# A 16-column projection in a two-block network kernel: rounded and low weight parts held side by side in one stationary tile

## The chip, the cores and the metric

The kernel runs on one core of one Trainium2 chip. The metric is device time in microseconds for one execution. Three executions of the kernel before took 2244.69, 2244.84 and 2245.06 us, so the median is 2244.84 us.

## What is computed

The reference runs two blocks over 512 tokens of width 1024. The first has two layers (Fourier and neighbourhood attention, a gated convolution, cross attention to a memory, a convolutional feed-forward part). The second has retention, a gated delta rule and a feed-forward part. The change touches only the two smallest of the second block's projections, `db` and `da`, 8 columns each:

```python
u = rmsnorm(h, g_mix[l])
proj = u @ w_in[l]
(..., db, da, gate_r, gate_d) = jnp.split(proj, split_at, axis=-1)
...
g = -jnp.exp(dn_a_log[l]) * jax.nn.softplus(da.astype(jnp.float32) + dn_dt_bias[l])
beta = jax.nn.sigmoid(db.astype(jnp.float32))
do = gated_delta_chunkwise(cq, ck, cv, g, beta)
```

`g` is summed up inside each chunk of 128 tokens, and its exponentials and `beta` weigh keys, queries and values in the delta rule.

## The kernel before

**Products.** Activations lie feature by token (128 x 512 tiles, eight of them for width 1024). Each fp32 product is made of three products of reduced operands: rounded weights by rounded activations, rounded weights by low activations, low weights by rounded activations. For activations the two parts are XH and XL, for weights w_hi and w_lo. One product is a weight load of 128 x 128 and a matmul that streams 512 tokens.

**Weights.** They come in units of 128 x 1024 floats through a ring of five slots. For each unit, in program order on each engine, SyncE loads w_raw when the unit five before it has been used (semaphore w_used, L492), ScalarE rounds it to w_hi (`split`, L689), and GpSimd subtracts to get w_lo (`lo`, L602; semaphore lo_done). TensorE waits on lo_done and runs `products`: 4 output tiles x 2 weight tiles x 3 products, 24 per unit (L1224).

**The projection.** Between the retention branch and the delta rule stands one unit named "dab". Its 128 stationary columns are 32 columns from `db` on, 32 from `da` on and 64 others, for each of eight weight tiles. Only columns 0 to 7 and 32 to 39 are read later. TensorE runs 8 x 3 products on it (L1841) into bank 0 of PSUM (tile ps) and counts w_used.

**The rows.** VectorE's `decay_rows` (L2284 to L2307) scales the two groups of 8 rows by the norm R, adds dt_bias, and with ScalarE's `decay_rows` (L1014 to L1026) makes beta (BR), the running sum GR of the decay, and two rows derived from it. ScalarE writes GR and BR to DRAM (L1027, L1028), waits until they have landed, and issues a load that spreads them over all 128 partitions (GB, `spread`, L1008). TensorE transposes the rows to columns in `decay_columns` (L1764), three units into the next group.

**The start of the delta rule.** TensorE goes on with four units for the keys (bank group A), four for the queries (bank group B), then `squares` (L1604), which needs ScalarE's SQk. VectorE's order there is fixed in code: `ages(0)` (L2348, L2352; needs GB), `evacuate(0)` (L2324), `with_beta(0)` (L2360), sixteen convolution taps on the keys (L2338, L2341), `ages(1)`, `evacuate(1)`. ScalarE follows with silu of the keys (L1051) and their squares SQk (L1055). The same order comes again for the second half of the heads, without the row computation.

Nothing is scheduled by a planner. Each engine's order is the order of the code, and semaphore values are written out by hand.

Of the kernel before, what the change touches and what calls it, by code (L numbers as in the profile page):

```python
# [18 lines left out]
F32 = mybir.dt.float32  # L19
F32R = mybir.dt.float32r  # L20
ACT = mybir.ActivationFunctionType
ALU = mybir.AluOpType
AX = mybir.AxisListType

P = 128
D = 1024
KT = D // P
T = 512
# [5 lines left out]
RING = 5  # L34
# [17 lines left out]
DN_H = 8  # L52
# [35 lines left out]
HALF = P // 2  # L88
# [6 lines left out]
def program(nc, ins, out):  # L95
    ctx = ExitStack()
    with ctx:
# [8 lines left out]
        XH = sb("XH", [P, KT, T], F32R)  # L106
        XL = sb("XL", [P, KT, T], F32R)
        w_raw = sb("w_raw", [P, RING, 2, UC])
        w_lo = nc.alloc_sbuf_tensor_at("w_lo", [P, RING, 2, UC], F32R, offset=nc.sbuf_base - RING * 2 * UC * 4)
        w_hi_at = nc.sbuf_base  # L110
        w_hi = sb("w_hi", [P, RING, 2, UC], F32R)
        R = sb("R", [P, T])
# [14 lines left out]
        ps = ctx.enter_context(nc.psum_tensor("ps", [P, 8, T], F32))  # L127

        def at(name, kb, shape, dt=F32):

            return nc.alloc_sbuf_tensor_at(name, shape, dt, offset=a0 + int(kb * KB))
# [36 lines left out]
        def pcol(name, i=0, n=1):  # L168
            c = PARAM_COLS[name][0] + i
            return par[:, c:c + n]  # L170
# [82 lines left out]
        SQo, LNo = at("SQo", 48, [P, 4, T]), at("LNo", 56, [P, 4, T])  # L253
        SQL, SQH = at("SQL", 48, [P, 4, T], F32R), at("SQH", 56, [P, 4, T], F32R)
        EGA = at("EGA", 88, [P, 4, T])
        GB = at("GB", TL + 25.5, [P, 2, 2, T])
        KD = at("KD", TL + 25.5, [P, 4, T])
        PKM, PKT = at("PKM", 64, [P, 4 * NCH, FIRST]), at("PKT", 65, [P, 4 * NCH, FIRST])
# [335 lines left out]
        def _(pool):  # L594
# [3 lines left out]
            def lo(u):  # L598

                s = u % RING  # L600
                pool.wait_ge(hi_done, u)
                nc.gpsimd.tensor_tensor(w_lo[:, s, :, :], w_raw[:, s, :, :], w_hi[:, s, :, :].bitcast(F32),  # L602
                                        ALU.subtract).then_inc(lo_done, 1)

# [77 lines left out]
        def _(act):  # L682
# [327 lines left out]
            def decay_rows():  # L1010

                B1, A1, A3, SPR, BEG, EGL, EG8 = [rows[i][:, :] for i in (0, 1, 2, 3, 4, 5, 6)]
                act.wait_ge(ab_dve, 1)
                nc.scalar.activation(BR[:, :], B1, ACT.Sigmoid).then_inc(ab_act, 1)  # L1014
                act.wait_ge(ab_dve, 3)
                nc.scalar.activation(A3, A1, ACT.Abs).then_inc(ab_act, 1)
                act.wait_ge(ab_act, 2)
                nc.scalar.activation(A3, A3, ACT.Exp, scale=-1.0).then_inc(ab_act, 1)
                act.wait_ge(ab_act, 3)
                nc.scalar.activation(A3, A3, ACT.Ln, bias=1.0).then_inc(ab_act, 1)  # L1020
                nc.scalar.activation(sm[0:DN_H, 80:81], pcol("a_log")[0:DN_H, :], ACT.Exp).then_inc(ab_act, 1)
                split_to(first["dab"] + 2 + LEAD)
                act.wait_ge(ab_dve, 9)
                nc.scalar.activation(EG8, GR[:, :], ACT.Exp).then_inc(ab_act, 1)
                act.wait_ge(ab_dve, 14)
                nc.scalar.activation(EGL, EGL, ACT.Exp).then_inc(ab_act, 1)  # L1026
                nc.scalar.dma_start(rows_dram[0], GR[:, :]).then_inc(rows_saved, 16)  # L1027
                nc.scalar.dma_start(rows_dram[1], BR[:, :]).then_inc(rows_saved, 16)  # L1028
                spread(0)
                split_to(first["dab"] + 3 + LEAD)  # L1030
                act.wait_ge(ab_t, 1)
                nc.scalar.activation(TC[:, :, :, :], ps[:, 1, 0:4 * NCH * DN_H].rearrange("p (a n h) -> p a n h", a=4, n=NCH),
                                     ACT.Copy).then_inc(ab_act, 1)
# [175 lines left out]
        def _(pe):  # L1209
# [547 lines left out]
            def decay_columns():  # L1757

                pe.wait_ge(ab_act, 7)
                pe.wait_ge(ab_dve, 14)  # L1760
                for a, row in enumerate((BR, GR, rows[4], rows[5])):
                    for n in range(NCH):
                        o = (a * NCH + n) * DN_H
                        mm = nc.tensor.transpose(ps[:, 1, o:o + DN_H], row[:, n * P:(n + 1) * P], ident[0:DN_H, 0:DN_H])  # L1764
                mm.then_inc(ab_t, 1)
# [55 lines left out]
            def block2():  # L1821
                u0 = first["rqk"]
                group(u0, 4, 0, XH, XL, x_ready("rqk"), after=stats("rqk"))
                stat_read("rqk")
                pe.wait_ge(bn_dve, 3)
                group(u0 + 4, 4, 4, XH, XL)
                for g in range(2):
                    pe.wait_ge(rqk_out, g + 1)
                    group(first["rv"] + 4 * g, 4, 4 * g, XH, XL, tokens_out=True)
                retention()  # L1830
                pair("gater", [[(ret_sc, 4 * RET_H)], [(ret_ro, 8)]])
                pair("retbr", [[(gr_dve, 1)], [(gr_dve, 2)]], YH, YL, lambda kt: [(rg_dve, 2 * (kt // 4) + 4)])

                u = first["dab"]
                pe.wait_ge(lo_done, u + 1)
                pe.wait_ge(rb_dve, 1)
                hi = w_hi[:, u % RING, :, :].rearrange("p a (b c) -> p (a b) c", c=P)
                lo = w_lo[:, u % RING, :, :].rearrange("p a (b c) -> p (a b) c", c=P)
                for kt in range(KT):
                    for n, (a, b) in enumerate(((hi, XH), (hi, XL), (lo, XH))):  # L1840
                        mm = nc.tensor.matmul(ps[:, 0, :], a[:, kt, :], b[:, kt, :], start=kt == 0 and n == 0,  # L1841
                                              stop=kt == KT - 1 and n == 2)
                mm.then_inc(w_used, 1)
                delta(0)
                delta(1)
                pair("dz", [[], [(do_ln, 2)]], after=out_stats(1))
                pair("dnbr", [[(dz_dve, 1)], [(dz_dve, 4)]], YH, YL, lambda kt: [(dz_dve, 3 * (kt // 4) + 3)])
                pair("wo2", [[(dn_dve, 1)], [(dn_dve, 4)]], NH, NL, lambda kt: [(dn_dve, 3 * (kt // 4) + 3)])
                ffn2()
                last_stats()  # L1850
# [5 lines left out]
        def _(dve):  # L1856
# [423 lines left out]
            def decay_rows():  # L2280
                B1, A1, A3, SPR, BEG, EGL, EG8, ONE = [rows[i][:, :] for i in range(8)]
                step = lambda n: dve.wait_ge(ab_dve, n)
                dve.wait_ge(w_used, first["dab"] + 1)
                nc.vector.tensor_tensor(B1, ps[0:DN_H, 0, :], R[0:DN_H, :], ALU.mult).then_inc(ab_dve, 1)  # L2284
                nc.vector.tensor_tensor(A1, ps[32:32 + DN_H, 0, :], R[32:32 + DN_H, :], ALU.mult).then_inc(ab_dve, 1)
                step(2)
                nc.vector.tensor_scalar(A1, A1, pcol("dt_bias")[0:DN_H, :], None, ALU.add).then_inc(ab_dve, 1)
                nc.vector.memset(ONE, 1.0)

                dve.wait_ge(ab_act, 4)  # L2290
                step(3)
                nc.vector.scalar_tensor_tensor(out=SPR, in0=A1, scalar=0.0, in1=A3, op0=ALU.max,
                                               op1=ALU.add).then_inc(ab_dve, 1)
                dve.wait_ge(ab_act, 5)
                step(4)
                nc.vector.tensor_scalar(SPR, SPR, sm[0:DN_H, 80:81], -1.0, ALU.mult, ALU.mult).then_inc(ab_dve, 1)
                step(5)
                for n in range(NCH):
                    c = slice(n * P, (n + 1) * P)
                    nc.vector.tensor_tensor_scan(GR[:, c], ONE[:, c], SPR[:, c], 0.0, ALU.mult, ALU.add).then_inc(ab_dve, 1)  # L2300
                step(9)
                for n in range(NCH):
                    c = slice(n * P, (n + 1) * P)
                    nc.vector.tensor_scalar(EGL[:, c], GR[:, c], GR[:, (n + 1) * P - 1:(n + 1) * P], -1.0,
                                            ALU.subtract, ALU.mult).then_inc(ab_dve, 1)
                dve.wait_ge(ab_act, 6)
                nc.vector.scalar_tensor_tensor(out=BEG, in0=EG8, scalar=-1.0, in1=BR[:, :], op0=ALU.mult,  # L2307
                                               op1=ALU.mult).then_inc(ab_dve, 1)
# [348 lines left out]
def lay_out(inputs):  # L2657
# [5 lines left out]
         "ret_g": feat(a["ret_norm_g_2"][0]), "dn_conv": feat(a["dn_conv_w_2"][0]), "dn_g": feat(a["dn_norm_g_2"][0]),  # L2663
         "ffn_w2": feat(a["ffn_conv_w_2"][0]), "ffn_b2": feat(a["ffn_conv_b_2"][0]),
         "a_log": np.pad(a["dn_a_log_2"].T, ((0, P - DN_H), (0, 0))),
         "dt_bias": np.pad(a["dn_dt_bias_2"].T, ((0, P - DN_H), (0, 0)))}
    for l in range(2):
        f[f"mix{l}"] = feat(a["mix_norm_g"][l])
        f[f"xa{l}"] = feat(a["xa_norm_g"][l])
# [9 lines left out]
    for n in WEIGHTS:  # L2679
# [5 lines left out]
WEIGHTS = ("w_in_ab", "w_out_ab", "w_in_c", "w_out_c", "xa_wq", "xa_wkv", "xa_wo", "ffn_w_up", "ffn_w_down",  # L2685
           "w_in_2", "w_ret_br_2", "w_dn_br_2", "w_o_2", "w_up_2", "w_down_2")
C_DB, C_DA, C_GR, C_GD = 7168, 7176, 7184, 8208
LOG_GAMMA = [float(np.log(1.0 - 2.0 ** (-5.0 - h))) for h in range(RET_H)]
SCALE_NA = float(P) ** -0.5
SCALE_X = float(2 * P) ** -0.5  # L2690
# [27 lines left out]
```

## Time and profile before

| quantity | value |
|---|---|
| median of three executions | 2244.84 us |
| span of the profiled execution | 2243.1 us |
| TensorE busy | 2224.7 us, 99% |
| VectorE, ScalarE, GpSimd busy | 952.6, 873.2, 1016.2 us |
| mean granted TensorE clock | 0.999 |
| waits of TensorE on the chain | 5% of the span is on other engines |

The span goes from the first to the last instruction of one profiled execution. The profile gives no other time for that execution; the median of the timed ones is 1.7 us longer than the span. A busy share says how much of the span the engine had an instruction under way. The chain of waits is followed back from the last instruction, each step to what released it.

### The profile page before, as it was taken

The numbers are of one execution on the slowest core, as the hardware profiler recorded it, in microseconds if no ns is written. First come the engines' busy times: TensorE is split into PE (matmuls) and PEld (weight loads), VectorE is DVE, ScalarE is ACT, GpSimd is POOL, SyncE is SP. The second block draws the span as 40 slices with busy tenths as digits, with TensorE's granted clock in tenths as the row PEclk, the third lists the DMA queues.
The fourth block names the chain that finished last, engine by engine and source line by source line (L and its number), as shares of the span: only waits on it lengthen the run. The fifth ranks groups of instructions, "written<-read, shape, count | busy, mean of one in ns | idle before, by whom it ended". The sixth has DMA issues, their size and how long they took to land.

```text
span 2243.1 us, 25574 instructions
## 1 busy us (share of the span) xinstructions
PE 2224.7 (99%) x10856; PEld 1836.8 (82%) x10856; DVE 952.6 (42%) x1171; ACT 873.2 (39%) x1080; POOL 1016.2 (45%) x431
## 2 busy tenths in 40 slices
PE   9999999999999999999999999999999999999998
PEld 7888878888888887888888877888878888888887
DVE  6251225342143403253414634168587224666603
ACT  4354334232322443332334536255664534332222
POOL 5427334444444472355443632434333454465643
PEclk9999999999999999999999999999999999999999
DMA  6215223323332341233233431344241233333322
GB/s 236 98 60 167 75 66 96 102 94 94 101 96 94 114 151 47 94 95 102 94 108 99 127 85 47 99 129 100 62 117 48 85 132 96 101 94 95 102 94 76
DMA packets 161090, 222.86 MB, mean 99 GB/s; under 512 B 24256, under 2 KB 87744, under 8 KB 160720
## 3 DMA queue, kind: packets, MB, share of 16 engines
q1 hardware_dynamic: 159136, 216.08, 31.0%
q10 hardware_dynamic: 1840, 5.15, 0.7%
q8 instruction: 86, 1.41, 0.3%
q14 instruction: 28, 0.23, 0.0%
HBM read 214.34 MB, written 6.85 MB: 99 GB/s over the span
## 4 chain that ended last, share of the span: by engine, by line
PE 95%; DVE 3%; ACT 1%; issue 0%; DMA 0%; POOL 0%; SPq 0%; DVEq 0%; ACTq 0%
PE ps L1224 82%; PE ps L1448 2%; PE ps L1461 1%; PE ps L1486 1%; PE ps L1445 1%; PE ps L1574 1%; PE ps L1310 1%; PE ps L1604 1%; PE ps L1563 0%; DVE ACC L1865 0%; PE ps L1619 0%; PE ps L1582 0%; PE ps L1631 0%; PE ps L1612 0%; PE ps L1474 0%
## 5 line engine op out<-in xcount | busy, mean ns | idle before, releaser
L602 POOL TENSOR_TENSOR w_lo<-w_raw,w_hi 128x1024 fp32r<-128x1024 f32 x378 | 972.8, 2583 | 1187.5 <-ACT w_hi L689 1172.1
L689 ACT ACTIVATE w_hi<-w_raw 128x1024 fp32r<-128x1024 f32 x378 | 396.2, 1056 | 885.2 <-DMA w_raw<-w_in 124.6
L1224 PE MATMUL ps<-XH,w_hi 128*128 128x512 f32 x1760 | 688.5, 391 | 0.0
L1224 PE MATMUL ps<-XH,w_lo 128*128 128x512 f32 x1760 | 685.0, 389 | 0.0
L1224 PE MATMUL ps<-XL,w_hi 128*128 128x512 f32 x1760 | 684.8, 389 | 0.0
L1224 PE MATMUL ps<-HID,w_hi 128*128 128x512 f32 x1728 | 533.1, 390 | 0.1
L1224 PEld LDWEIGHTS ps<-XH,w_hi 128*128 128x128 f32 x1760 | 330.4, 188 | 69.5 <-issue 1.2
L1224 PEld LDWEIGHTS ps<-XH,w_lo 128*128 128x128 f32 x1760 | 330.3, 188 | 69.3
L1224 PEld LDWEIGHTS ps<-XL,w_hi 128*128 128x128 f32 x1760 | 330.4, 188 | 68.8 <-issue 1.2
L1224 PEld LDWEIGHTS ps<-HID,w_hi 128*128 128x128 f32 x1728 | 324.2, 188 | 68.4 <-issue 1.0
L1224 PE MATMUL ps<-HID,w_lo 128*128 128x512 f32 x864 | 336.1, 389 | 0.0
L1224 PEld LDWEIGHTS ps<-HID,w_lo 128*128 128x128 f32 x864 | 162.2, 188 | 33.8
L1889 DVE TENSOR_TENSOR H<-ps,H 128x512 f32<-128x512 f32 x60 | 39.7, 683 | 307.9 <-PE ps L1224 307.9
L2132 DVE TENSOR_TENSOR GP<-ps,R 128x1024 f32<-128x1024 f32 x16 | 19.6, 1225 | 176.3 <-PE ps L1224 176.3
L2083 DVE TENSOR_TENSOR QX<-ps,R 128x2048 f32<-128x2048 f32 x4 | 9.2, 2292 | 156.4 <-PE ps L1224 156.4
L1865 DVE TENSOR_TENSOR ACC<-ACC,SQ 128x512 f32<-128x512 f32 x59 | 48.1, 815 | 42.1 <-ACT SQ L699 38.2
L2520 DVE SCALAR_TENSOR_TENSOR CV<-GP,par,CV 128x512 f32<-128x512 f32 x88 | 65.7, 817 | 0.0
L2512 DVE TENSOR_TENSOR GP<-ps,R 128x2048 f32<-128x2048 f32 x11 | 25.2, 2292 | 75.8 <-PE ps L1224 75.8
L912 ACT ACTIVATE EG<-CV,par 128x512 f32<-128x512 f32 x32 | 22.2, 725 | 85.6 <-DVE CV L2141 85.6
L699 ACT ACTIVATE SQ<-H 128x512 f32<-128x512 f32 x52 | 32.8, 631 | 32.3 <-DVE ACC L1865 21.9
L2141 DVE SCALAR_TENSOR_TENSOR CV<-GP,par,CV 128x512 f32<-128x512 f32 x64 | 43.6, 740 | 0.0
L2150 DVE TENSOR_TENSOR HID<-HF,HID 128x1024 fp32r<-128x1024 f32 x16 | 35.5, 2221 | 18.1 <-ACT HID L916 18.1
(398 smaller groups left out, 2228.5 us busy)
## 6 DMA issues: line engine op xcount, KB each, us to landing
w_raw<-w_in SPq DMA_DIRECT2D x72, 512.0 KB, 3.8
w_raw<-ffn_w_up SPq DMA_DIRECT2D x128, 256.0 KB, 2.9
w_raw<-w_up SPq DMA_DIRECT2D x88, 256.0 KB, 3.0
w_raw<-xa_wkv SPq DMA_DIRECT2D x32, 512.0 KB, 3.7
w_raw<-ffn_w_down SPq DMA_DIRECT2D x32, 512.0 KB, 3.8
w_raw<-w_in_c SPq DMA_DIRECT2D x24, 512.0 KB, 3.8
w_raw<-w_down SPq DMA_DIRECT2D x22, 512.0 KB, 3.7
w_raw<-xa_wq SPq DMA_DIRECT2D x16, 512.0 KB, 3.8
```

The lines of the kernel that those rows point to most:

```text
L602: nc.gpsimd.tensor_tensor(w_lo[:, s, :, :], w_raw[:, s, :, :], w_hi[:, s, :, :].bitcast(F32), ALU.subtract).then_inc(lo_done, 1)
L689: nc.scalar.activation(w_hi[:, s, :, :], w_raw[:, s, :, :], ACT.Copy).then_inc(hi_done, 1)
L699: nc.scalar.activation(ACC[:, :] if c == 0 else SQ[:, :], H[:, c, :], ACT.Square).then_inc(sq_done, 1)
L1224: mm = nc.tensor.matmul(ps[:, bank + m, :], a, b, start=start and j == 0 and n == 0, stop=stop and j == 1 and n == 2)
L1310: mm = nc.tensor.matmul(ps[:, m, :], wt, (XL if n == 1 else XH)[:, kt, :], start=False, stop=k == 3 and n == 2 and j == 1)
L1448: mm = nc.tensor.matmul(ps[:, bank + m, :], xt[:, m * P:(m + 1) * P], wt, start=begin, stop=end)
L1865: nc.vector.tensor_tensor(ACC[:, :], ACC[:, :], SQ[:, :], ALU.add).then_inc(acc_done, 1)
L1889: nc.vector.tensor_tensor(H[:, c, :], ps[:, (c + flip) % 8, :], H[:, c, :], ALU.add).then_inc(h_upd, 1)
L2141: nc.vector.scalar_tensor_tensor(out=CV[:, q, :], in0=GP[:, q, i:T + i], scalar=tap(i, q), in1=CV[:, q, :], op0=ALU.mult, op1=ALU.add).the ...
L2150: nc.vector.tensor_tensor(HID[:, 2 * g + nf:2 * g + nf + 2, :], HF[:, :, :], HID[:, 2 * g:2 * g + 2, :].bitcast(F32), ALU.subtract).then_i ...
L2512: nc.vector.tensor_tensor(GP4[:, :, 2:T + 2], banks(bank), over(R[:, :], 4), ALU.mult).then_inc(up2_dve, 1)
L2520: nc.vector.scalar_tensor_tensor(out=CV4[:, q, :], in0=GP4[:, q, i:T + i], scalar=of(w0 + 2 * nf * i, q), in1=CV4[:, q, :], op0=ALU.mult, ...
```

## The change

GpSimd no longer writes w_lo for the unit "dab". It subtracts only for the first 64 columns of each of the eight weight tiles, and writes the result into columns 64 to 127 of w_hi, over rounded weights that nobody reads. TensorE then runs two products per weight tile, XH and XL, over the 128 columns of w_hi: rows 0 to 39 of ps hold the rounded weights' share, rows 64 to 103 the low weights' share. The product of low weights by low activations, left out before, is now included. VectorE scales both groups of 40 rows (ABL, ABH) and adds them: `db` by a tensor_tensor, `da` together with dt_bias by a scalar_tensor_tensor that takes the place of the tensor_scalar. dt_bias moves to partitions 32 to 39 of the parameter tile. Every later value of the semaphore ab_dve grows by one, and ScalarE's sigmoid waits for the third VectorE step where it waited for the first.

```diff
+        ABH, ABL = at("ABH", 80, [DAB_ROWS, T]), at("ABL", 82, [DAB_ROWS, T])
...
                 pool.wait_ge(hi_done, u)
+                if u == first["dab"]:
+                    raw, hi = [w[:, s, :, :].rearrange("p a (b c) -> p (a b) c", c=P) for w in (w_raw, w_hi)]
+                    nc.gpsimd.tensor_tensor(hi[:, :, HALF:P], raw[:, :, 0:HALF], hi[:, :, 0:HALF].bitcast(F32),
+                                            ALU.subtract).then_inc(lo_done, 1)
+                    return
...
-                act.wait_ge(ab_dve, 1)
+                act.wait_ge(ab_dve, 3)
                 nc.scalar.activation(BR[:, :], B1, ACT.Sigmoid).then_inc(ab_act, 1)
-                act.wait_ge(ab_dve, 3)
+                act.wait_ge(ab_dve, 4)
                 nc.scalar.activation(A3, A1, ACT.Abs).then_inc(ab_act, 1)
...
-                hi = w_hi[:, u % RING, :, :].rearrange("p a (b c) -> p (a b) c", c=P)
-                lo = w_lo[:, u % RING, :, :].rearrange("p a (b c) -> p (a b) c", c=P)
+                both = w_hi[:, u % RING, :, :].rearrange("p a (b c) -> p (a b) c", c=P)
                 for kt in range(KT):
-                    for n, (a, b) in enumerate(((hi, XH), (hi, XL), (lo, XH))):
-                        mm = nc.tensor.matmul(ps[:, 0, :], a[:, kt, :], b[:, kt, :], start=kt == 0 and n == 0,
-                                              stop=kt == KT - 1 and n == 2)
+                    for n, x in enumerate((XH, XL)):
+                        mm = nc.tensor.matmul(ps[:, 0, :], both[:, kt, :], x[:, kt, :], start=kt == 0 and n == 0,
+                                              stop=kt == KT - 1 and n == 1)
...
-                nc.vector.tensor_tensor(B1, ps[0:DN_H, 0, :], R[0:DN_H, :], ALU.mult).then_inc(ab_dve, 1)
-                nc.vector.tensor_tensor(A1, ps[32:32 + DN_H, 0, :], R[32:32 + DN_H, :], ALU.mult).then_inc(ab_dve, 1)
+                low = slice(HALF, HALF + DAB_ROWS)
+                nc.vector.tensor_tensor(ABL[:, :], ps[low, 0, :], R[low, :], ALU.mult).then_inc(ab_dve, 1)
+                nc.vector.tensor_tensor(ABH[:, :], ps[0:DAB_ROWS, 0, :], R[0:DAB_ROWS, :], ALU.mult).then_inc(ab_dve, 1)
                 step(2)
-                nc.vector.tensor_scalar(A1, A1, pcol("dt_bias")[0:DN_H, :], None, ALU.add).then_inc(ab_dve, 1)
+                nc.vector.tensor_tensor(B1, ABH[0:DN_H, :], ABL[0:DN_H, :], ALU.add).then_inc(ab_dve, 1)
+                nc.vector.scalar_tensor_tensor(out=A1, in0=ABH[32:DAB_ROWS, :], scalar=pcol("dt_bias")[32:DAB_ROWS, :],
+                                               in1=ABL[32:DAB_ROWS, :], op0=ALU.add, op1=ALU.add).then_inc(ab_dve, 1)
                 nc.vector.memset(ONE, 1.0)
```

On TensorE, from the last products of the retention branch (HID) into the unit "dab" and the second weight tile of it, the order before is this:

```order
L1224 MATMUL ps<-HID,w_lo 128x512
L1841 MATMUL ps<-XH,w_hi 128x512 [waits rb_dve,lo_done]
L1841 MATMUL ps<-XL,w_hi 128x512
L1841 MATMUL ps<-XH,w_lo 128x512
L1841 MATMUL ps<-XH,w_hi 128x512
L1841 MATMUL ps<-XL,w_hi 128x512
```

and now:

```order
L1230 MATMUL ps<-HID,w_lo 128x512
L1846 MATMUL ps<-XH,w_hi 128x512 [waits rb_dve,lo_done]
L1846 MATMUL ps<-XL,w_hi 128x512
L1846 MATMUL ps<-XH,w_hi 128x512
L1846 MATMUL ps<-XL,w_hi 128x512
```

The product with w_lo is gone from each of the eight weight tiles; what stands ahead of the unit, what follows it and what it waits for are as before.

On VectorE, from the last product of the retention branch's gate (MG) to the first chunk of the running sum, the order before is this (row_144 is the `db` row, row_145 the `da` row):

```order
L2571 TENSOR_TENSOR MG<-MG,ps 128x2048 [waits gr_act,w_used] x2
L2284 TENSOR_TENSOR row_144<-ps,R 8x512 [waits w_used]
L2285 TENSOR_TENSOR row_145<-ps,R 8x512
L2287 TENSOR_SCALAR row_145<-row_145,par 8x512 [waits ab_dve]
L2288 MEMSET row_151 8x512
L2292 SCALAR_TENSOR_TENSOR row_147<-row_145,row_146 8x512 [waits ab_dve,ab_act]
L2296 TENSOR_SCALAR row_147<-row_147,sm 8x512 [waits ab_dve,ab_act]
L2300 SCALAR_TENSOR_TENSOR GR<-row_151,row_147 8x128 [waits ab_dve]
```

and now (row_146 is the `db` row, row_147 the `da` row):

```order
L2579 TENSOR_TENSOR MG<-MG,ps 128x2048 [waits gr_act,w_used] x2
L2290 TENSOR_TENSOR ABL<-ps,R 40x512 [waits w_used]
L2291 TENSOR_TENSOR ABH<-ps,R 40x512
L2293 TENSOR_TENSOR row_146<-ABH,ABL 8x512 [waits ab_dve]
L2294 SCALAR_TENSOR_TENSOR row_147<-ABH,par,ABL 8x512
L2296 MEMSET row_153 8x512
L2300 SCALAR_TENSOR_TENSOR row_149<-row_147,row_148 8x512 [waits ab_dve,ab_act]
L2304 TENSOR_SCALAR row_149<-row_149,sm 8x512 [waits ab_dve,ab_act]
L2308 SCALAR_TENSOR_TENSOR GR<-row_153,row_149 8x128 [waits ab_dve]
```

The `db` row was ready after the first of three instructions and the `da` row after the third; now they are ready after the third and the fourth of four.

## Rows read from the trace of the kernel before

**Rows 1.** The page: span, and busy time of each engine with its instruction count.

```profile
span 2243.1 us, 25574 instructions
PE 2224.7 (99%) x10856; PEld 1836.8 (82%) x10856; DVE 952.6 (42%) x1171; ACT 873.2 (39%) x1080; POOL 1016.2 (45%) x431
```

**Rows 2.** The page: the chain that ended last, by engine.

```profile
PE 95%; DVE 3%; ACT 1%; issue 0%; DMA 0%; POOL 0%; SPq 0%; DVEq 0%; ACTq 0%
```

**Rows 3.** Chain of waits, 1440 to 1560 us: start, duration, what.

```profile
1455.83 5.44 PE ps L1841 x24
1461.27 16.32 PE ps L1224 x72
1477.59 1.08 PE ps L1764 x16
1478.67 27.43 PE ps L1224 x120
```

**Rows 4.** Timeline of GpSimd, the unit dab: start, duration, line, tiles, idle before and releaser.

```profile
1440.00 2.39 POOL L602 TENSOR_TENSOR w_lo<-w_raw,w_hi 128x1024 fp32r<-128x1024 f32 x1 [4.10 <-ACT w_hi L689]
```

**Rows 5.** Timeline of VectorE, 1455 to 1512 us.

```profile
1455.87 2.29 DVE L2571 TENSOR_TENSOR MG<-MG,ps 128x2048 f32<-128x2048 f32 x1 [19.47 <-PE ps L1224]
1461.31 0.68 DVE L2284 TENSOR_TENSOR row<-ps,R 8x512 f32<-8x512 f32 x1 [3.15 <-PE ps L1841]
1462.02 0.68 DVE L2285 TENSOR_TENSOR row<-ps,R 8x512 f32<-8x512 f32 x1
1462.73 0.63 DVE L2287 TENSOR_SCALAR row<-row,par 8x512 f32<-8x512 f32 x1
...
1482.91 1.04 DVE L2348 TENSOR_TENSOR DL<-GB,TC 128x512 f32<-128x512 f32 x1 [2.22 <-DMA GB<-rows_dram]
1483.98 0.69 DVE L2352 SCALAR_TENSOR_TENSOR DL<-DL,cst 128x512 f32<-128x512 f32 x1
1484.59 0.69 DVE L2348 TENSOR_TENSOR DL<-GB,TC 128x512 f32<-128x512 f32 x1
...
1493.57 7.96 DVE L2341 SCALAR_TENSOR_TENSOR KN<-ps,par,KN 128x511 f32<-128x511 f32 x12
...
1506.14 2.29 DVE L2324 TENSOR_TENSOR H<-ps,R 128x2048 f32<-128x2048 f32 x1 [1.96 <-PE ps L1224]
```

**Rows 6.** Timeline of ScalarE and its DMA issues, 1455 to 1604 us.

```profile
1475.02 0.63 ACT L1026 ACTIVATE row<-row 8x512 f32<-8x512 f32 x1 [0.87 <-DVE row L2307]
...
1477.06 0.40 ACTq L1008 DMA_DIRECT2D GB<-rows_dram  x1
...
1501.56 1.92 ACT L1051 ACTIVATE KN<-KN 128x2048 f32<-128x2048 f32 x1 [5.66 <-DVE KN L2341]
1503.51 1.92 ACT L1055 ACTIVATE SQk<-KN 128x2048 f32<-128x2048 f32 x1
...
1531.82 1.92 ACT L1055 ACTIVATE SQq<-QN 128x2048 f32<-128x2048 f32 x1
```

**Rows 7.** Timeline of TensorE's weight loads in three stretches.

```profile
1505.71 0.42 PEld L1604 LDWEIGHTS ps<-SQk,cst 128*128 128x128 f32 x2
...
1534.54 0.42 PEld L1604 LDWEIGHTS ps<-SQq,cst 128*128 128x128 f32 x2
...
1571.32 0.54 PEld L1646 LDWEIGHTS ps<-MM,AT 64*64 64x64 f32 x16 [0.92 <-DVE MM L2458]
```

**Rows 8.** Timeline of VectorE, 1508 to 1604 us.

```profile
1557.43 0.69 DVE L2428 TENSOR_TENSOR ATT<-ps,DL 128x512 f32<-128x512 f32 x1 [0.91 <-PE ps L1631]
...
1570.82 0.45 DVE L2458 STREAM_TRANSPOSE MM<-MTP 128x256 f32<-128x256 f32 x1
```

**Rows 9.** SyncE's issue of the weights nearest to GB's.

```profile
1477.62 0.37 SPq L492 DMA_DIRECT2D w_raw<-w_in  x1
```

**Rows 10.** All four loads of GB (L1008): issue to landing.

```profile
DMA to landing us min/median/max: 4.9/6.1/7.2
```

**Rows 11.** The stretch from 1482 us on: busy shares, granted clock, DMA share, GB/s.

```profile
1482.00:1483.00 1.00, 1.00 (x6) 0.84 (x5) 0.09 (x1) 0.09 (x1) 1.00 (x1) 1.00 0.94 367
```

More of the change, by code:

```diff
@@ L1022, in decay_rows @@
                 split_to(first["dab"] + 2 + LEAD)
-                act.wait_ge(ab_dve, 9)
+                act.wait_ge(ab_dve, 10)
                 nc.scalar.activation(EG8, GR[:, :], ACT.Exp).then_inc(ab_act, 1)
-                act.wait_ge(ab_dve, 14)
+                act.wait_ge(ab_dve, 15)
                 nc.scalar.activation(EGL, EGL, ACT.Exp).then_inc(ab_act, 1)
@@ L1759, in decay_columns @@
                 pe.wait_ge(ab_act, 7)
-                pe.wait_ge(ab_dve, 14)
+                pe.wait_ge(ab_dve, 15)
                 for a, row in enumerate((BR, GR, rows[4], rows[5])):
@@ L2283, in decay_rows @@
                 dve.wait_ge(w_used, first["dab"] + 1)
-                nc.vector.tensor_tensor(B1, ps[0:DN_H, 0, :], R[0:DN_H, :], ALU.mult).then_inc(ab_dve, 1)
-                nc.vector.tensor_tensor(A1, ps[32:32 + DN_H, 0, :], R[32:32 + DN_H, :], ALU.mult).then_inc(ab_dve, 1)
+                low = slice(HALF, HALF + DAB_ROWS)
+                nc.vector.tensor_tensor(ABL[:, :], ps[low, 0, :], R[low, :], ALU.mult).then_inc(ab_dve, 1)
+                nc.vector.tensor_tensor(ABH[:, :], ps[0:DAB_ROWS, 0, :], R[0:DAB_ROWS, :], ALU.mult).then_inc(ab_dve, 1)
                 step(2)
-                nc.vector.tensor_scalar(A1, A1, pcol("dt_bias")[0:DN_H, :], None, ALU.add).then_inc(ab_dve, 1)
+                nc.vector.tensor_tensor(B1, ABH[0:DN_H, :], ABL[0:DN_H, :], ALU.add).then_inc(ab_dve, 1)
+                nc.vector.scalar_tensor_tensor(out=A1, in0=ABH[32:DAB_ROWS, :], scalar=pcol("dt_bias")[32:DAB_ROWS, :],
+                                               in1=ABL[32:DAB_ROWS, :], op0=ALU.add, op1=ALU.add).then_inc(ab_dve, 1)
                 nc.vector.memset(ONE, 1.0)
                 dve.wait_ge(ab_act, 4)
-                step(3)
+                step(4)
                 nc.vector.scalar_tensor_tensor(out=SPR, in0=A1, scalar=0.0, in1=A3, op0=ALU.max,
@@ L2294, in decay_rows @@
                 dve.wait_ge(ab_act, 5)
-                step(4)
+                step(5)
                 nc.vector.tensor_scalar(SPR, SPR, sm[0:DN_H, 80:81], -1.0, ALU.mult, ALU.mult).then_inc(ab_dve, 1)
-                step(5)
+                step(6)
                 for n in range(NCH):
@@ L2300, in decay_rows @@
                     nc.vector.tensor_tensor_scan(GR[:, c], ONE[:, c], SPR[:, c], 0.0, ALU.mult, ALU.add).then_inc(ab_dve, 1)
-                step(9)
+                step(10)
                 for n in range(NCH):
@@ L2665, in lay_out @@
          "a_log": np.pad(a["dn_a_log_2"].T, ((0, P - DN_H), (0, 0))),
-         "dt_bias": np.pad(a["dn_dt_bias_2"].T, ((0, P - DN_H), (0, 0)))}
+         "dt_bias": np.pad(a["dn_dt_bias_2"].T, ((32, P - 32 - DN_H), (0, 0)))}
     for l in range(2):
@@ L2687 @@
 C_DB, C_DA, C_GR, C_GD = 7168, 7176, 7184, 8208
+DAB_ROWS = 32 + DN_H
 LOG_GAMMA = [float(np.log(1.0 - 2.0 ** (-5.0 - h))) for h in range(RET_H)]
```

## The prediction, on record before the changed kernel ran

> **What bounds the kernel.** I read the page first. TensorE is busy 99% of the span, no other engine over half of it [rows 1], and the chain that ended last runs on TensorE for 95% of the span [rows 2]. So the kernel is as long as TensorE's stream, and a change pays by what it takes out of that stream and costs by the waits that it puts in. Then I read the chain of waits around the change. The 24 products of the unit "dab" take 5.44 us, and the chain goes through them and on into the next group without a gap [rows 3]. 5.44 / 24 = 0.227 us for one product, and the ordinary products behind them go at the same pace: 16.32 us for 72, again 0.227. A single product's record is longer than that, since products overlap; the pace is what counts. Last I read the timelines of VectorE, ScalarE and the weight loads, for how late each result comes to those who need it. All steps below are counted from the end of "dab" on TensorE, 1461.27 us before [rows 3]; the change itself brings that end forward.
>
> **What is removed on TensorE.** Eight products of 0.227 us: 8 x 5.44 / 24 = 1.81 us. The remaining sixteen stream the same 512 tokens against the same 128 columns, so I price them at the pace of the 24. The low weights' columns ride along with the rounded ones at no cost.
>
> The Trainium skill, page "TensorE: Matmul & The Clock Gate", section "Back-to-back issue gap", gives for a stream of weight-load and matmul pairs at 512 columns a sustained spacing of about 131 ns. By that rule, as an estimate, eight products would be worth 1.05 us, and the whole change 0.65 us. This trace has 227 ns, so the measurement decides.
>
> **What is added ahead of TensorE.** GpSimd's subtraction becomes half as large. The one for "dab" ends at 1440.00 + 2.39 = 1442.4 us [rows 4], and its unit is used from 1455.83 us on: 13.4 us of cover. Even a strided write as slow as a whole tile, or three times that, stays hidden. The units behind are loaded when the unit five before is released, so their slack of some 13 us shrinks by at most the 1.81 us that "dab" gets shorter. VectorE ends the retention gate's product at 1455.87 + 2.29 = 1458.2 us [rows 5], which the next group needs; "dab" will end at 1459.46 us, so 1.3 us of cover are left. I cost all of this at nothing.
>
> **What is added behind it.** Before, the `da` row is ready at 1462.73 + 0.63 = 1463.36 us, 2.05 us after VectorE started on the rows [rows 5]. Now four instructions stand there. The first two go at 0.71 us from start to start, as the old pair did (1461.31, 1462.02, 1462.73 [rows 5]); that there are 40 partitions in place of 8 costs nothing, because instructions on 128 partitions and 512 elements take 0.69 us too (L2352 [rows 5]). Sum and scalar_tensor_tensor at 0.71 each make 3 x 0.71 + 0.69 = 2.82 us, so the `da` row comes 0.77 us later. The sigmoid now waits for the third instruction but ends at 2.76 us, before the `da` row is there, so it adds nothing. From here ScalarE's exponential and logarithm, VectorE's running sum and the last exponential (L1026) each wait for the one before, so the whole chain is 0.77 us later.
>
> The Trainium skill, page "VectorE: DVE Perf Modes", section "Two Vector instructions with no wait between them", says that an instruction whose input starts in another quadrant of 32 partitions than that of the last instruction is held until all earlier ones have finished. The new fourth instruction reads from partition 32. Held, it starts 0.71 us behind the third; not held, it could start 0.61 us behind, as L2348 behind L2352 does (1483.98 to 1484.59 [rows 5]), and the delay would be 0.67 us.
>
> Who waits for it? First `decay_columns` on TensorE, at 1477.59 us [rows 3]. The last exponential ends at 1475.02 + 0.63 = 1475.65 us [rows 6]. Of these 1.94 us of slack 1.17 are left, no wait.
>
> Second the spread load of GB. It is issued at 1477.06 us, lands at about 1482.9 us, and both VectorE (idle 2.22 us) and ScalarE sit waiting for it [rows 5, 6]. Then VectorE has no gap until 1501.53 us (1493.57 + 7.96 [rows 5]), ScalarE follows with silu and squares, and SQk is there at 1503.51 + 1.92 = 1505.43 us [rows 6]. TensorE loads the weights of the first `squares` product at 1505.71 us [rows 7]. A wait on this engine holds back the weight load: the one at 1571.32 us starts 0.05 us after VectorE's transpose ends at 1570.82 + 0.45 = 1571.27 us [rows 7, 8]. So this join has 1505.71 - 1505.43 - 0.05 = 0.23 us of slack. It is the tightest place of the change. If GB lands s later, TensorE waits s - 0.23 us here.
>
> What is s? The issue is 0.77 us later. Before, GB (1024 KB) was issued 0.56 us ahead of a weight unit (1477.62 us [rows 9]), and together they filled the DMA engines until 1483 us (94% busy in the last microsecond [rows 11]). Now the weight unit goes first, at the same time after "dab", and GB behind it. The sum of bytes is the same and starts to move about half a microsecond later, so GB may land only 0.5 us later; with no such sharing it is the full 0.77. Bounds for the wait are thus 0.27 and 0.54 us from the carried delay; 0 if the delay is swallowed in the load. I take 0.4 us, the middle of the two bounds with a delay, since VectorE and ScalarE both stand idle for this load.
>
> Does it cost again later? The next needs are SQq, ready at 1531.82 + 1.92 = 1533.74 us and needed at 1534.54 us [rows 6, 7], slack 0.75 us, and VectorE's ATT products, where it idles 0.91 us for TensorE [rows 8]. TensorE itself is then 0.4 us later, so both hold. VectorE's evacuation of the queries is released by TensorE (idle 1.96 us [rows 5]) and does not see the delay. The second half of the heads reads rows that have long been there.
>
> **Sum.** 1.81 removed, 0.40 added: 1.41 us less. The span goes from 2243.1 to about 2241.7 us, and the time, which lies 1.7 us above the span, from the median 2244.84 to 2243.4 us, 0.06% less. A difference under 0.2%, 4.5 us here, is about what a measurement of this kernel can't tell from no change; I count it as the same.
>
> **Rivals.**
> *The delay is hidden.* If GB's landing shifts by 0.23 us or less, because its packets share the DMA engines with the weight unit anyway, all 1.81 us stay: 2243.0 us. The full DMA share speaks for it; against it that VectorE and ScalarE both stand idle for GB.
> *GB's load becomes the wait, and the kernel slower.* Four such loads take 4.9 to 7.2 us to land, this one 5.8 [rows 5, 6, 10]. Behind a weight unit it may take the longest: s = 0.77 + 1.4 = 2.17 us, a wait of 1.94 us, and 0.13 us lost in all: 2245.0 us. It decides from s over 2.04 us on. Against it: the bytes in flight are the same.
> *Nothing arrives.* If what TensorE gains is given back at a wait tied to something that does not move, the time stays 2244.8 us. TensorE has waits on VectorE in the inverse and the chain's DMA share is 0% [rows 2]; those waits start from TensorE's own results and move with it. I see no such anchor.
>
> **Chances.** Forecast 2243.4 us: 0.60; hidden, 2243.0: 0.25; nothing arrives, 2244.8: 0.08; slower by GB, 2245.0: 0.04; something unseen over 4.5 us either way: 0.03. The range holds the first two with the measured spread of 0.4 us and reaches toward the others: 2242.5 to 2244.5 us. Every case but the last lies within 0.2%: same 0.95, faster 0.03, slower 0.02.
>
> **What would show it.** Right: the 16 products take 3.63 us; the `da` row is ready 2.8 us after the first row instruction; the weight load of the first `squares` starts 0.05 us after SQk ends and shows a wait on ScalarE of 0.3 to 0.5 us; everything behind 1510 us lies about 1.4 us earlier. Wrong: a pace other than 0.227 us, a wait at `decay_columns` or at a weight unit, row instructions slower on 40 partitions, or GB landing earlier after its issue than 5.3 us or later than 6.5.

## The result, and the profile after

The changed kernel takes 2247.45 us (median of 20 runs), the kernel before 2244.99 us (20 runs beside it). The medians differ by 2.5 us, 0.11%. The ratio of the means is 1.0013, 95% interval [1.0007, 1.0019], so the kernel is slower, clear of the noise. That lies within 0.2%, as forecast, but with the other sign and outside the range of 2242.5 to 2244.5 us. Fourteen of the runs lie between 2247.0 and 2247.8 us, five between 2248.6 and 2250.6 us. One more, at 2473 us, was disturbed and is left out of the comparison.

The products did what was expected. From the chain of waits of the changed kernel, start, duration, what (against [rows 3]):

```profile
1456.23 3.64 PE ps L1846 x16
1459.90 0.69 DVE ABL L2290
1460.62 0.69 DVE ABH L2291
1461.34 2.68 DVE row L2293
1464.05 0.75 DVE row L2294
...
1477.02 3.07 DMA rows_dram<-BR
1480.11 4.92 DMA GB<-rows_dram
1485.05 1.96 DVE DL L2356
...
1506.54 1.93 ACT SQk L1061
1508.61 3.67 PE ps L1610 x8
```

Sixteen products take 3.64 us, 1.80 less than the 24. But the chain, which before stayed on TensorE all through this stretch, now leaves it at the end of the unit and comes back 49 us later at the squares. In between it is VectorE, ScalarE and DMA that set the end. The list of TensorE's waits has two new entries (who waits, for whom, total, times, longest):

```profile
PE ps L1610 <- ACT SQk L1061: 1.3, 1, 1.3
...
PE ps L1770 <- ACT row L1032: 0.9, 1, 0.9
```

VectorE's timeline shows where the rows are lost (against the first rows of [rows 5]):

```profile
1459.90 0.69 DVE L2290 TENSOR_TENSOR ABL<-ps,R 40x512 f32<-40x512 f32 x1 [1.34 <-PE ps L1846]
1460.62 0.68 DVE L2291 TENSOR_TENSOR ABH<-ps,R 40x512 f32<-40x512 f32 x1
1461.34 2.68 DVE L2293 TENSOR_TENSOR row<-ABH,ABL 8x512 f32<-8x512 f32 x1
1464.05 0.74 DVE L2294 SCALAR_TENSOR_TENSOR row<-ABH,par,ABL 8x512 f32<-8x512 f32 x1
```

and GpSimd's beside it:

```profile
1461.08 2.39 POOL L608 TENSOR_TENSOR w_lo<-w_raw,w_hi 128x1024 fp32r<-128x1024 f32 x1 [3.03 <-ACT w_hi L695]
```

The first sum takes 2.68 us where 0.7 was expected. It starts 0.26 us after GpSimd's subtraction for a weight unit and ends 0.55 us after that one's end at 1463.47 us. Both scaled groups lie in SBUF: it is VectorE's first instruction on the rows whose two tensor operands both come from there. The instruction ahead of it ran under the same subtraction for its last 0.22 us, but reads one operand from PSUM (ps), and took 0.68 us.

The two stretches behind the wait at the transposes show the granted clock (last but two of the numbers):

```profile
1478.00:1480.00 2.00, 2.00 (x10) 1.65 (x10) 0.00 (x0) 0.00 (x0) 0.00 (x0) 0.64 0.67 236
1480.00:1482.00 2.00, 2.00 (x7) 1.51 (x6) 0.00 (x0) 1.45 (x3) 0.31 (x1) 0.51 0.35 137
```

TensorE stood for 0.95 us, and then its clock was at the lower level, 1.2 GHz, over most of these 4 us: eight products at 0.425 us in place of 0.227, some 1.6 us. Before, the clock was 1.00 here.

Counted from the end of the unit (1461.27 us before, 1456.23 + 3.64 = 1459.87 after), SQk ended 44.16 us behind it before, and 48.60 us now. The 4.4 us are (the steps from the `da` row to the last exponential took 11.7 us both times):

| step | before | after | more |
|---|---|---|---|
| first row instruction to `da` row ready | 2.05 | 4.89 | 2.84 |
| last exponential's start to GB's issue | 2.04 | 3.67 | 1.63 |
| GB's issue to VectorE's first use | 5.85 | 4.94 | -0.91 |
| first VectorE instruction on GB | 1.04 | 1.95 | 0.91 |

Less 0.23 us of slack and the 1.8 us of products this makes the squares start some 2.4 us later. They did not themselves take longer: from their first weight load to their end 3.83 us before (1505.71 to 1509.54 us) and 3.70 us now (1508.58 to 1512.28 us). Their row in the chain of the kernel before:

```profile
1506.10 3.44 PE ps L1604 x8
```

The same from the start of the unit (1455.83 and 1456.23 us) to the end of the squares: 53.71 us before, 56.05 us after, 2.3 us more, against 2.5 us measured. The profile of the changed kernel is 2.8 us longer than the one before. 0.4 us of that lie ahead of the unit, where the start of the unit scatters between 1455.6 and 1456.2 us over the profiles of all runs.

### The profile page after: what moved, and what is told of

It is laid out like the page before. It is cut to its first block, busy times and chain, and to the rows that moved or that the text cites. A ratio compares the mean times of both kernels' runs of the same rounds, so it can differ in the third digit from the quotient of the medians.

```text
span 2245.9 us, 25559 instructions
## 1 busy us (share of the span) xinstructions
PE 2226.8 (99%) x10848; PEld 1838.4 (82%) x10848; DVE 953.5 (42%) x1172; ACT 872.7 (39%) x1080; POOL 1009.9 (45%) x431
## 4 chain that ended last, share of the span: by engine, by line
PE 94%; DVE 4%; ACT 1%; DMA 1%; issue 0%; POOL 0%; DVEq 0%; SPq 0%; ACTq 0%
PE ps L1230 80%; PE ps L1454 2%; PE ps L1467 1%; PE ps L1492 1%; PE ps L1451 1%; PE ps L1580 1%; PE ps L1316 1%; PE ps L1610 1%; PE ps L1569 0%; DVE KN L2349 0%; PE ps L1303 0%; PE ps L1625 0%; PE ps L1588 0%; PE ps L1637 0%; PE ps L1618 0%
```

## The experiments

Theory: (1) an instruction of VectorE with both tensor operands in SBUF stands until GpSimd's running subtraction has ended; (2) the shorter unit brings the rows under such a subtraction; (3) the save of the rows then shares the DMA engines with a weight unit; (4) the lost time ends in the wait for SQk. Rivals: partitions and start partition of the sum; the shared tile by itself; the wait at the transposes with its low clock. Each time below is the median of 11 runs (e11: one run); "before" is the kernel before on the same chip. The ratios are those of the means.

**e1, the products alone.** The low rows are not added, so beta and decay miss that share.

```diff
-                nc.vector.tensor_tensor(ABL[:, :], ps[low, 0, :], R[low, :], ALU.mult).then_inc(ab_dve, 1)
...
+                nc.vector.tensor_tensor(B1, ps[0:DN_H, 0, :], R[0:DN_H, :], ALU.mult).then_inc(ab_dve, 2)
+                nc.vector.tensor_tensor(A1, ps[32:32 + DN_H, 0, :], R[32:32 + DN_H, :], ALU.mult).then_inc(ab_dve, 1)
+                step(3)
+                nc.vector.tensor_scalar(A1, A1, pcol("dt_bias")[0:DN_H, :], None, ALU.add).then_inc(ab_dve, 1)
```

> 16 products as in the changed kernel, but VectorE's three old instructions on rows 0 to 7 and 32 to 39; the low weights' rows are not added, so that share is left out of beta and decay. Theory (the products are worth their pace, and the loss sits on VectorE and behind it): 3.63 us for the 16, no wait at the column transposes, no fall of TensorE's clock, time before minus 1.8 us, 2243.2. Rival (16 products on the shared tile, or the earlier end of the unit by itself, upset the weight supply or the clock): a low clock or a wait in front of the row transposes also here, time within 0.5 us of before or above it.

Measured: 2245.34 us (2242.88 to 2248.98), before 2244.77, ratio 1.0005 [0.9996, 1.0013]. The expectation of 2243.2 us failed. VectorE's timeline of this run:

```profile
1460.14 0.68 DVE L2291 TENSOR_TENSOR row<-ps,R 8x512 f32<-8x512 f32 x1
1460.86 2.38 DVE L2293 TENSOR_SCALAR row<-row,par 8x512 f32<-8x512 f32 x1
```

GpSimd beside it, and GpSimd at this place in the kernel before:

```profile
1460.57 2.40 POOL L608 TENSOR_TENSOR w_lo<-w_raw,w_hi 128x1024 fp32r<-128x1024 f32 x1 [3.09 <-ACT w_hi L695]
...
1460.68 2.39 POOL L602 TENSOR_TENSOR w_lo<-w_raw,w_hi 128x1024 fp32r<-128x1024 f32 x1 [2.87 <-ACT w_hi L689]
```

Even the old tensor_scalar, with a single tensor operand, from SBUF to SBUF, now stands for GpSimd (1460.57 + 2.40 = 1462.97 us; it ends 0.27 us later). Before it had begun at 1462.73 us, 0.34 us ahead of the subtraction's end at 1463.07 us, and took 0.63 us [rows 5], ending 0.29 us behind it. So taking 1.8 us off TensorE alone moves VectorE by 1.8 us into a wait of 1.9 us. In the profile GB also took 6.8 us to its first use, where it took 5.85 us before (its first instruction took 0.69 us in place of 1.04), and TensorE waited at the squares, not at the transposes:

```profile
PE ps L1610 <- ACT SQk L1061: 1.8, 1, 1.8
```

So the rival was right in its second half: the earlier end of the unit by itself costs what it saves, above all by VectorE, with some of it from GB's load; the clock stayed at 1.00 through this profile's wait. Of the eleven runs only one came at the 1.8 us that the products are worth. Four came at 2246.8 us or more; none of these was profiled.

**e2, one operand of each sum in PSUM.**

```diff
-                nc.vector.tensor_tensor(ABH[:, :], ps[0:DAB_ROWS, 0, :], R[0:DAB_ROWS, :], ALU.mult).then_inc(ab_dve, 1)
+                nc.vector.tensor_tensor(ps[0:DAB_ROWS, 2, :], ps[0:DAB_ROWS, 0, :], R[0:DAB_ROWS, :], ALU.mult).then_inc(ab_dve, 1)
...
-                nc.vector.tensor_tensor(B1, ABH[0:DN_H, :], ABL[0:DN_H, :], ALU.add).then_inc(ab_dve, 1)
+                nc.vector.tensor_tensor(B1, ps[0:DN_H, 2, :], ABL[0:DN_H, :], ALU.add).then_inc(ab_dve, 1)
```

> The changed kernel, but the scaled rounded share stays in PSUM, so each of the two adding instructions reads one operand from SBUF and one from PSUM. Theory (an instruction with both tensor operands in SBUF stands until GpSimd's running subtraction ends): the first sum takes 0.7 us in place of 2.68, the rows are 2 us earlier, no wait at the column transposes, clock stays at 1.0, GB is loaded 2 us or more earlier, a short wait of 0.3 to 0.6 us at the squares, time 2243.3 to 2243.7. Rival (the sum was long because of the 40 partitions or of the start at partition 32): 2.7 us again and 2247.4.

Measured: 2243.61 us (2243.44 to 2243.79), before 2244.77 (2244.44 to 2245.27), ratio 0.9995 [0.9986, 1.0004]. The scalar_tensor_tensor was edited in the same way. VectorE and, beside it, GpSimd:

```profile
1460.71 0.68 DVE L2293 TENSOR_TENSOR row<-ps,ABL 8x512 f32<-8x512 f32 x1
1461.42 0.74 DVE L2294 SCALAR_TENSOR_TENSOR row<-ps,par,ABL 8x512 f32<-8x512 f32 x1
```

```profile
1460.44 2.40 POOL L608 TENSOR_TENSOR w_lo<-w_raw,w_hi 128x1024 fp32r<-128x1024 f32 x1 [2.97 <-ACT w_hi L695]
```

The same sum, from the same partitions, under the same subtraction, takes 0.68 us, and the product that is written to PSUM 0.69 us. The save takes 1.45 us, there is no wait at the transposes, the clock stays at 1.00, and TensorE's wait for SQk is short:

```profile
PE ps L1610 <- ACT SQk L1061: 0.3, 1, 0.3
```

**e3, GpSimd held back.** Operands as in the changed kernel.

```diff
+                elif u == first["dab"] + 4:
+                    pool.wait_ge(ab_dve, 4)
```

> The changed kernel with one wait more on GpSimd: its subtraction for the fourth unit behind the 16-column one starts only after VectorE's fourth row instruction. Operands and partitions are as in the changed kernel. Theory (GpSimd's running subtraction holds the sum): sum 0.7 us, everything behind as in the run with the sum in PSUM, 2243.3 to 2243.7. Rival (partitions or operands in themselves): sum 2.7 us, 2247.4.

Measured: 2243.69 us (2243.34 to 2244.16), ratio 0.9996 [0.9987, 1.0004]. VectorE:

```profile
1460.69 0.68 DVE L2295 TENSOR_TENSOR row<-ABH,ABL 8x512 f32<-8x512 f32 x1
```

GpSimd:

```profile
1462.21 2.40 POOL L608 TENSOR_TENSOR w_lo<-w_raw,w_hi 128x1024 fp32r<-128x1024 f32 x1 [4.76 <-DVE row L2296]
```

Two operands in SBUF are not slow in themselves, nor are 40 partitions or a start at partition 32. Only together with GpSimd's subtraction do they cost 2 us. e2 and e3 take away one side each, and the sum takes 0.68 us both times; (1) is shown, and the first rival falls. The wait for SQk was 0.8 us in e3's profile and 0.3 us in e2's: GB took 6.7 us to its first use here and 6.2 us there, issued 0.3 us behind a weight unit in both.

The Trainium skill, page "SBUF — State Buffer", section "SBUF: two separate sides", says that VectorE and GpSimd contend for one pair of SBUF ports, that it is an exclusive lock and not a split of bandwidth, and that VectorE needs it in a 2-port mode or with two SBUF inputs. The runs agree: 2.68 us with the lock held, 0.68 us with an operand in PSUM or GpSimd at rest.

**e4 and e11, the transposes one weight unit later.** TensorE runs `decay_columns` after the fourth unit.

```diff
-                    if after is not None and k == 2:
+                    if after is not None and k == after_k:
...
+                after=decay_columns if q == 0 else out_stats(0), after_k=3 if q == 0 else 2)
```

> The changed kernel, but TensorE transposes the rows to columns after the fourth unit of the keys and not after the third, 5.4 us later. Theory A (the late GB sets the end; the 0.95 us wait and the 1.7 us of low clock behind it are covered by the later wait for the key squares): no wait of 0.95 us, no low clock there, but 3 to 4 us of waiting at the squares, time as the changed kernel, 2247.0 to 2248. Theory B (wait and low clock are on the path, 2.6 us together): 2244.8 to 2245.2.

Measured: 2248.37 us (2246.76 to 2249.56), before 2244.77, ratio 1.0015 [1.0006, 1.0024]; four runs at 2246.8 to 2247.2, six at 2248.0 to 2248.6, one at 2249.6. The median lies above the range of either theory. TensorE's waits in the profile, a run of the first group:

```profile
PE ps L1610 <- ACT SQk L1061: 3.4, 1, 3.4
```

The wait at the transposes and the low clock there are gone, and nothing is won: the wait at the squares has grown from 1.3 to 3.4 us. From the start of the unit to the end of the squares this profile has 56.03 us, the changed kernel's 56.05 us. Theory A holds for the first group. In the changed kernel the 0.95 us wait and the 1.6 us of low clock lie in front of SQk, which would not have been there earlier. The second group needed another profile.

> The kernel with the transposes later once more, for one more profile: its times lay at 2246.8 to 2247.2 and at 2248.0 to 2248.6, and the profile seen so far is of the first group. Theory (the two groups differ by whether TensorE's clock falls behind its 3.4 us wait at the squares): if this run is near 2248.4, the clock is at half in 1508 to 1514 us and products there take 0.43 us; if it is near 2247, the clock is at 1.0 there. Rival (another place makes the second group): near 2248.4 and the clock at 1.0 throughout that stretch.

Measured: 2248.91 us, one run, nearest to the second group (before on this chip 2245.03 us). Chain and stretch of it:

```profile
1508.15 5.37 PE ps L1610 x8
```

```profile
1510.00:1512.00 2.00, 2.00 (x3) 0.67 (x2) 0.55 (x1) 1.99 (x5) 1.38 (x1) 0.50 0.00 0
```

Behind its wait of 3.5 us the clock is at the lower level, and the squares take 5.37 us in place of 3.67: 1.7 us, now on the path. The theory on the groups holds. The wait alone doesn't decide it: the profile of e4 has a wait of 3.4 us and a clock of 1.00. Of the changed kernel's five slower runs, the two at 2248.6 and 2249.1 us could be such falls behind its second wait. The three at 2250.5 us lie 3.1 us above the others, more than one fall cost. None of the five was profiled, and their cause stays open.

**e5, the row save ahead of the weight unit; e6, saves and GB ahead of it.** Both keep the slow sum.

```diff
+                        if u == first["dab"] + 8:
+                            sp.wait_ge(rows_saved, 32)    # e5
+                            sp.wait_ge(gb_loaded, 16)     # e6, in its place
```

> The changed kernel, but SyncE issues the weight unit that started just ahead of the two row saves only when both saves have landed. The sum still stands for GpSimd. Theory A (the save landed 1.6 us late because it shared the DMA engines with that unit, and this is on the path): save to GB issue 1.5 us in place of 3.1, GB at VectorE 1 us or more earlier, 2246.0 to 2246.6. Theory B (GB then shares with the unit instead, and the 1.6 us come back in GB's landing, 6 to 6.7 us in place of 4.9): within 0.4 us of the changed kernel, 2247.0 to 2247.8.

> As the last, but the weight unit waits until GB has landed, so saves and GB both have the DMA engines for themselves; the unit has over 10 us of slack. Theory (the sum's 2 us and the DMA sharing together make the loss): save 1.5 us, GB 4.5 to 5 us, SQk 1.5 us earlier than in the changed kernel, 2245.6 to 2246.2. Rival (the low clock of 1.7 us after the wait at the transposes sets the end then, since it stays): TensorE arrives at the squares after SQk and the time is 2246.2 to 2247.4, with no wait there.

Measured: e5 2246.67 us (2246.41 to 2248.54), ratio 1.001 [1.0001, 1.0018]; e6 2245.64 us (2245.33 to 2246.36), ratio 1.0003 [0.9994, 1.0012]; before 2244.94. Chains of e5 and e6:

```profile
1476.68 1.43 DMA rows_dram<-BR
1478.13 6.78 DMA GB<-rows_dram
```

```profile
1476.53 1.43 DMA rows_dram<-BR
1477.97 5.17 DMA GB<-rows_dram
```

The save takes 1.43 us where it took 3.07, so it was the weight unit, issued ahead of it, that delayed it. In e5 GB then shares with that unit and needs 6.78 us: save and load together 8.2 us, in the changed kernel 8.0. Theory B holds for the DMAs, while the time lies between the two ranges. Four of e5's runs came at 2247.9 to 2248.5 us; its profile is of the faster seven. The 0.8 us by which e5 is faster nevertheless came one step on: VectorE's first instruction on GB took 0.69 us, since it no longer met a subtraction (1.95 us in the changed kernel). In e6 both DMAs are free and 1.4 us are saved there; with 1.8 us less than the changed kernel it came in at the forecast. Its rival was not put to the test: the profile has the wait of 1.1 us at the transposes, but a clock of 1.00 behind it. In e5 the same wait of 1.1 us was followed by a clock of 0.50, and TensorE was ready for the squares 1.6 us later than in e6. As an estimate from the two profiles, with such a fall TensorE would have come to e6's squares 0.3 us after SQk. The stretch from 1478 us on in e5 and in e6:

```profile
1478.00:1480.00 2.00, 2.00 (x5) 1.61 (x6) 0.00 (x0) 1.35 (x3) 0.21 (x1) 0.50 0.37 40
```

```profile
1478.00:1480.00 2.00, 2.00 (x10) 1.62 (x10) 0.09 (x1) 1.58 (x3) 0.45 (x1) 1.00 0.44 133
```

**e7, 24 products on the shared tile.**

```diff
+                    mm = nc.tensor.matmul(ps[:, 3, :], both[:, kt, :], XH[:, kt, :], start=kt == 0, stop=kt == KT - 1)
```

> The changed kernel with eight products more: the shared tile by XH once more into an unused bank, so the unit takes 24 products as before and its rows start 1.8 us later. Theory (the sum collides with GpSimd's subtraction only because the unit got shorter): the sum takes 0.7 to 1.0 us, not 2.7; rows, save and GB about 1 us later than before, a wait of 0.5 to 1.0 us at the squares, 2245.3 to 2245.9, which is less than the changed kernel's 2247.4 in spite of 1.8 us more of products. Rival (the sum is slow wherever it stands): 2.7 us and 2248 or more.

Measured: 2245.97 us (2245.61 to 2246.83), before 2244.94, ratio 1.0005 [0.9996, 1.0014]. VectorE:

```profile
1462.62 1.05 DVE L2294 TENSOR_TENSOR row<-ABH,ABL 8x512 f32<-8x512 f32 x1
```

GpSimd:

```profile
1460.73 2.39 POOL L608 TENSOR_TENSOR w_lo<-w_raw,w_hi 128x1024 fp32r<-128x1024 f32 x1 [3.23 <-ACT w_hi L695]
```

With 1.8 us more work on TensorE the kernel is faster than the changed one: the rows start later, the sum meets only the last half microsecond of the subtraction and again ends 0.55 us behind it. (2) is shown. The wait at the squares was 1.2 us, more than the 0.5 to 1.0 expected, because GB took 6.8 us, issued behind a weight unit.

**e8, sum in PSUM and GB ahead of the weight unit.**

> The version that the runs so far point to: one operand of each sum in PSUM, and the weight unit behind GB. Theory: sums 0.7 us, save 1.5 us, GB lands 4.5 to 5 us after its issue, no wait at the squares, all 1.8 us of the removed products arrive: 2242.8 to 2243.2. Rival (the delayed unit or what comes behind it now waits, or GB does not land sooner): 2243.4 to 2243.8 as without that step, or more.

Measured: 2243.78 us (2243.33 to 2243.97), before 2244.94, ratio 0.9994 [0.9985, 1.0003]. The time is the rival's, for a cause that it did not name: GB was there 5.35 us after its issue, against 6.20 in e2, but the first instruction on it ran into GpSimd's two subtractions.

```profile
1481.70 1.51 DVE L2358 TENSOR_TENSOR DL<-GB,TC 128x512 f32<-128x512 f32 x1 [2.00 <-DMA GB<-rows_dram]
```

**e9, e1 with GpSimd held back** as in e3 (low share left out, as in e1).

> As the run with the products alone (16 products, VectorE's three old instructions, the low weights' share left out), but GpSimd's subtraction for the fourth unit behind starts only after the rows' third VectorE instruction. Theory (that run came out at 2245.3 and scattered by 6 us only because the shorter unit pushed the tensor_scalar, both of whose ports are in SBUF, under GpSimd's subtraction, 2.38 us in place of 0.5): tensor_scalar 0.5 us, no wait at the squares, 2242.9 to 2243.2 with little scatter. Rival (the earlier unit costs elsewhere too, as in the load of GB): 2243.4 or more.

Measured: 2243.15 us (2242.81 to 2243.52), before 2245.03 (2244.58 to 2245.39), ratio 0.9992 [0.9983, 1.0001]. The tensor_scalar takes 0.48 us, nothing waits at the squares, and the removed products are worth 1.9 us against 1.81 computed. The scatter of e1 is gone with the collision: 0.7 us over eleven runs, against 6.1 us.

**e10, e8 with GpSimd's seventh subtraction behind VectorE's work on GB.**

```diff
+                elif u == first["dab"] + 7:
+                    pool.wait_ge(dp_pre, 4)
```

> The version with the sum in PSUM and the weight unit behind GB, and one wait more on GpSimd: its subtraction for the seventh unit behind the 16-column one starts after VectorE's four instructions on GB. Theory (there the first instruction on GB stood 0.8 us for GpSimd, which gave back what the earlier landing won): that instruction takes 0.69 us, SQk is 0.8 us earlier, no wait at the squares, 2242.9 to 2243.3. Rival (the next pair of VectorE's instructions then stands longer for GpSimd, or the late subtraction holds TensorE): 2243.6 or more.

Measured: 2243.43 us (2242.87 to 2243.60), before 2245.03 (2244.58 to 2245.39), ratio 0.9992 [0.9984, 1.0001]. The first instruction on GB:

```profile
1481.24 0.69 DVE L2360 TENSOR_TENSOR DL<-GB,TC 128x512 f32<-128x512 f32 x1 [1.88 <-DMA GB<-rows_dram]
```

The time lies between the ranges of theory and rival. The first instruction is as fast as the theory said, but VectorE's next pair that meets GpSimd took longer, as the rival said: the two products into AT (L2372) took 3.60 us together, 3.00 us in e8. SQk ended 0.3 us earlier than in e8, counted from the end of the unit, and not 0.8. Nothing waited at the squares.

This is the complete computation, 1.6 us faster than before and 4 us faster than the changed kernel. The interval of the ratio just touches 1; all eleven runs lie below all 21 of before. e2, with a single edit, has 1.2 of the 1.6 us.

## Why the prediction was wrong

- *What bounds the kernel, and the products.* Right: 3.64 us for sixteen, 1.8 us less, and e9 turns them into 1.9 us of time.
- *"Sum and scalar_tensor_tensor at 0.71 each."* This step failed. The sum took 2.68 us. The 0.71 came from the old pair, which read one operand from PSUM and, like the sum in e2, ran under a subtraction without standing for it; the sum reads both from SBUF. Where it did not meet GpSimd (e3) it took 0.68 us, so only the collision was missing. Signs stood in the prediction's own groups: the first instruction on GB took 1.04 us where its twin took 0.69, and the tensor_scalar 0.63 us [rows 5] where the one at L2296 takes 0.48. Larger ones stood in the same trace. The same instruction on GB, for the second half of the heads, and GpSimd beside it:

```profile
1606.68 2.55 DVE L2348 TENSOR_TENSOR DL<-GB,TC 128x512 f32<-128x512 f32 x1 [6.36 <-DMA GB<-rows_dram]
...
1606.28 2.40 POOL L602 TENSOR_TENSOR w_lo<-w_raw,w_hi 128x1024 fp32r<-128x1024 f32 x1 [27.91 <-ACT w_hi L689]
```

It ends 0.55 us behind the subtraction, as the sum does. The fourth instruction was priced right: it started 0.71 us behind the third in e2 and 0.70 us in e3. I did not ask what GpSimd was doing at the new time of each instruction.
- *"I cost all of this at nothing"*, of GpSimd and the weight units. Right for what TensorE waits for, wrong as a whole. The subtraction that meets the rows stays fixed to the units before (it started at 1460.4 to 1461.1 us in every profile where it was not held back), while the rows move 1.8 us forward under it. e3 and e7 show the price, 2 us on VectorE.
- *`decay_columns`: "no wait".* 1.17 us of slack against 2 us more: a wait of 0.95 us, and in the profile 1.6 us lost at half clock behind it. e4 shows that in this kernel both are covered by the wait for SQk.
- *The load of GB.* That it shares with a weight unit was seen, that the save would was not: with rows 2.8 us late the save of 16 KB fell behind the weight unit (3.07 us for 1.46), and GB was then faster. e5 shows that for the DMAs the two even out.
- *The tightest join.* Right in place, the squares, with 0.23 us of slack. The delay there was 4.4 us and not 0.6. Where the sum is free of GpSimd, the wait is 0.3 us and the time 2243.6 us (e2), or 0.8 us and 2243.7 us (e3), against 0.4 us and 2243.4 us in the forecast. That e2 comes so close is in part luck: counted from the end of the unit, GB came into use 1.2 us later than before and not 0.8 at most, and its first instruction, which met no subtraction, gave 0.35 us back.
- *The rival on the slower side* had the end right, a late GB and a wait for SQk, but not the cause; GB itself took 4.9 us, the least of the range that it named, and outside the 5.3 to 6.5 us that the prediction gave as its own sign.
- *A difference under 0.2% "can't be told from no change".* The 0.11% lies within 0.2%, as said, but it could be told: the interval [1.0007, 1.0019] leaves 1 out.

## What to carry to other kernels

When a change shortens the critical engine, everything that hangs on it moves forward against engines whose work is fixed to earlier events: lay the other engines' rows over the new times, not the old. For an instruction of VectorE that reads SBUF twice, or a tensor_scalar from SBUF to SBUF, look for GpSimd's instructions at the same time, and read an outlier of a known shape as a collision. In e2 keeping one operand in PSUM cost no time (0.69 and 0.68 us) and took the instruction out of it.

## What the runs showed that I had not expected

- A sum of 8 x 512 took 0.68 us free and 2.68 us under a subtraction of GpSimd's of 2.39 us; it ended 0.53 to 0.55 us after that one in all six profiles where they met (the changed kernel, e4, e5, e6, e7, e11). A tensor_scalar of one tensor operand was held as well (2.38 against 0.48 us). A sum and a scalar_tensor_tensor with one operand in PSUM were not (0.68 and 0.74 us).
- A wait of TensorE of 0.95 to 1.1 us was followed by a clock of 1.2 GHz in the changed kernel and e5, and not in e6; one of 3.4 to 3.5 us was in e11 and not in e4. A fall cost 1.6 us (changed kernel) and 1.7 us (e11). The same kernel goes both ways.
- The second of two saves of 16 KB took 1.43 to 1.45 us in e1, e2, e3, e5, e6, e7 and e8, and 2.84 to 3.07 us when a 512 KB load had been issued 0.24 to 0.25 us ahead of the first (the changed kernel, e4, e11). In e1 that load was issued 0.21 us behind the second save, which still took 1.43 us.
- The row chain seems to hold one more such stand in every kernel here, the one before included. Before, one of the four steps of the running sum (L2300, both operands in SBUF) took 2.54 us, the other three 0.39 to 0.41, and it ran under the subtraction at 1470.45 us; the four together took 3.5 us in every profile. No run has this step free of GpSimd, so that it stands for it is not shown.
